# Attention B of three row blocks: head outputs kept turned, halves aligned by DMA, summed and scaled on GpSimd

## What is computed

```
score = sum_h w[t,h] * relu(q_idx[t,h] . k_idx[s])       # indexer
idx   = top_k(score, 256)                                # per row
logits[q,h,k] = q[h] . k[idx] / 8 + bias;  p = softmax(logits)
o_b   = p @ v                                            # 8 heads x 64
merged = sigmoid(gate_a) * (o_a @ w_branch_a) + sigmoid(gate_b) * (o_b @ w_branch_b)
x = x + merged @ w_out;  x = x + SwiGLU(rmsnorm(x));  out = rmsnorm(x)
```

## Time and profile before

| | before |
|---|---|
| median of 3 runs | 3301.77 us (3299.1 to 3305.61) |
| profiled execution | 3303.4 us, its span 3301.5 us |
| PE busy in the span | 3218.6 us, 97% |
| DVE, ACT, POOL busy | 59%, 44%, 55% |
| mean granted TensorE clock | 0.995 |

### The profile page before, as it was taken

One profiled execution on the slowest core, in us unless ns is written; L12 is line 12 of the kernel. 1 busy time (PEld: TensorE's weight loads), 2 busy tenths in 40 slices (PEclk: granted clock), 3 DMA queues, 4 the chain that ended last, 5 costly groups with the idle time before them and its releaser, 6 DMA issues.

```text
span 3301.5 us, 43302 instructions
## 1 busy us (share of the span) xinstructions
PE 3218.6 (97%) x15976; PEld 2698.9 (82%) x15976; DVE 1937.2 (59%) x3494; ACT 1441.6 (44%) x2610; POOL 1809.6 (55%) x1261
## 2 busy tenths in 40 slices
PE   8999999999999999999999999999999999999998
PEld 6888878878888888888888888888888789888887
DVE  3236747648565656567676766767868778621112
ACT  3324435435453544345454535736655367420001
POOL 5555554454455666645666664166666721566665
PEclk9999999999999999999999999999999999999999
DMA  5745454355524333323433332063333400433332
GB/s 160 204 138 173 115 165 138 105 152 154 190 79 147 108 112 97 118 90 120 162 103 107 96 119 93 1 233 100 101 96 116 157 18 1 137 118 96 96 102 96
DMA packets 446561, 388.98 MB, mean 118 GB/s; under 512 B 20976, under 2 KB 376560, under 8 KB 445712
## 3 DMA queue, kind: packets, MB, share of 16 engines
q1 hardware_dynamic: 424912, 341.99, 34.0%
q10 hardware_dynamic: 21440, 44.22, 3.6%
HBM read 323.37 MB, written 62.78 MB: 117 GB/s over the span
## 4 chain that ended last, share of the span: by engine, by line
PE 88%; DVE 4%; ACT 3%; POOL 2%; issue 2%; DMA 1%; ACTq 0%; SPq 0%; DVEq 0%; POOLq 0%
PE BANK L913 20%; PE BANK L914 20%; PE BANK L915 20%; PE LP L913 3%; PE LP L914 3%; PE LP L915 3%; PE BANK L1138 3%; PE LP L1122 2%; PE BANK L1153 2%; PE LP L1023 2%; PE LP L1022 2%; PE LP L1123 2%; PE BANK L1155 2%; POOL WLO L863 1%; PE BANK L1164 1%
## 5 line engine op out<-in xcount | busy, mean ns | idle before, releaser
L863 POOL TENSOR_TENSOR WLO<-WRAW,WHI 128x1024 fp32r<-128x1024 f32 x456 | 1107.1, 2428 | 38.0
L861 POOL TENSOR_SCALAR WHI<-WRAW 128x1024 fp32r<-128x1024 f32 x456 | 506.4, 1111 | 1036.7 <-PE BANK L915 846.0
L913 PE MATMUL BANK<-H2hi,WHI 128*128 128x512 f32 x1376 | 542.9, 395 | 6.8 <-ACT SL L1716 4.4
L914 PE MATMUL BANK<-H2lo,WHI 128*128 128x512 f32 x1376 | 538.4, 391 | 0.0
L915 PE MATMUL BANK<-H2hi,WLO 128*128 128x512 f32 x1376 | 537.7, 391 | 0.0
L913 PE MATMUL BANK<-HThi,WHI 128*128 128x512 f32 (+1 forms) x1024 | 404.5, 395 | 2.6 <-DVE QS L1782 2.6
L914 PE MATMUL BANK<-HTlo,WHI 128*128 128x512 f32 (+1 forms) x1024 | 400.0, 391 | 0.0
L915 PE MATMUL BANK<-HThi,WLO 128*128 128x512 f32 (+1 forms) x1024 | 400.0, 391 | 0.0
L1515 ACT ACTIVATE MASK<-SCD,THR 128x896 bf16<-128x896 f32 (+5 forms) x186 | 281.9, 1516 | 249.0 <-DVE THR L1842 221.4
L913 PEld LDWEIGHTS BANK<-H2hi,WHI 128*128 128x128 f32 x1376 | 259.9, 189 | 60.4 <-ACT SL L1716 4.8
L915 PEld LDWEIGHTS BANK<-H2hi,WLO 128*128 128x128 f32 x1376 | 259.6, 189 | 55.5
(11 more groups left out here) (294 smaller groups left out, 6666.8 us busy)
## 6 DMA issues: line engine op xcount, KB each, us to landing
WRAW<-in_w_in SPq DMA_DIRECT2D x124, 512.0 KB, 4.4
WRAW<-in_w_ffn_gate SPq DMA_DIRECT2D x88, 512.0 KB, 3.8
WRAW<-in_w_ffn_up SPq DMA_DIRECT2D x88, 512.0 KB, 3.8
WRAW<-in_w_ffn_down SPq DMA_DIRECT2D x88, 512.0 KB, 3.5
qsp<-QS SPq DMA_DIRECT2D x32, 512.0 KB, 5.7
gates<-GS ACTq DMA_DIRECT2D x64, 256.0 KB, 2.2
WRAW<-in_w_out SPq DMA_DIRECT2D x32, 512.0 KB, 4.2
GL<-gates ACTq DMA_DIRECT2D x48, 256.0 KB, 4.3
```

The lines of the kernel that those rows point to most:

```text
L861: nc.gpsimd.tensor_scalar(hi, raw, 1.0, 1.0, ALU.mult, ALU.mult).then_inc(w_hi, 1)
L863: nc.gpsimd.tensor_tensor(lo, raw, hi.bitcast(f32), ALU.subtract).then_inc(w_split, 1)
L913: nc.tensor.matmul(dst, whi, mhi, start=first, stop=False)
L914: nc.tensor.matmul(dst, whi, mlo, start=False, stop=False)
```

## The change

For blocks 1 to 3 the turn to [rows, d] and back falls away. XV stays in [d, rows]. Four SP DMAs for each quad (`shift_halves`) bring the half that lies in the wrong partitions to XZ and the half that is in place to OTB; POOL adds the two and multiplies by the inverted sums (`fold`). The sums lie in [rows, heads] and are needed along the free axis in all 64 partitions of a head: one DMA writes them to memory (`hand_sums`), two more read them back as a broadcast (`load_sums`). The last quad takes another way: ACT copies its upper half to the lower partitions, and DVE adds and scales it (`fold_last`). `sums_at` sets the slots of `whole_sums` and `invert` before the end of the quad. Block 0 stays as it was.

```diff
+        LASTQ = PAIRS // 2 - 1
+        def sums_at(b, kind, q):
+            if b == 0:
+                return quad_end(b, kind, q) + 2
+            count = len(groups(b, kind, 2 * q + 1))
+            return first_at(b, kind, 2 * q + 1) + (4 if count > 6 else 3 if count > 4 else 1)
...
+            def hand_sums(b, q):
+                j, g = q // 2, q % 2
+                sp.wait_ge(inverted, n(inverted, (b, "b", q)))
+                made(sum_out, (b, q), 16)
+                sp.dma_start(io["rsd"][b, j, 4 * g:4 * g + 4, :].rearrange("h r -> r h"), RS[:, j, 4 * g:4 * g + 4],
+                             allow_slow_non_contiguous=True).then_inc(sum_out, 16)
+            def load_sums(b, q):
+                j, g = q // 2, q % 2
+                sp.wait_ge(sum_out, n(sum_out, (b, q)))
+                if q >= 2:
+                    sp.wait_ge(o_scaled, n(o_scaled, (b, q - 2)))
+                made(sum_in[q % 2], (b, q), 32)
+                for s in range(2):
+                    sp.dma_start(RR[q % 2][s * HD:(s + 1) * HD, :, :],
+                                 io["rsd"][b, j, 4 * g:4 * g + 4, :].rearrange("(e s) r -> s e r", s=2)[s].partition_broadcast(HD)
+                                 ).then_inc(sum_in[q % 2], 16)
+            def shift_halves(b, q):
+                sp.wait_ge(x_copied, n(x_copied, (b, "b", q)))
+                if q >= 2:
+                    sp.wait_ge(o_scaled, n(o_scaled, (b, q - 2)))
...
+                for s in range(2):
...
+                    sp.dma_start(XZ[q % 2][r, :, :], other).then_inc(x_shifted[q % 2], 16)
+                    sp.dma_start(OTB[r, 2 * g:2 * g + 2, j * P:(j + 1) * P], own).then_inc(x_shifted[q % 2], 16)
...
                 if key == ("br", b, 1, 1):
+                    for q in range(LASTQ - 1) if b else ():
+                        hand_sums(b, q)
+                        load_sums(b, q)
+                        shift_halves(b, q)
                     last = units(b, "b")[-1]
                     sp.wait_ge(masked, n(masked, (last, chunks_of(last)[-1][0])))
...
+                    if b:
+                        hand_sums(b, LASTQ - 1)
+                        load_sums(b, LASTQ - 1)
+                        shift_halves(b, LASTQ - 1)
+                        hand_sums(b, LASTQ)
+                        load_sums(b, LASTQ)
...
+                def fold(q):
+                    j, g, s = q // 2, q % 2, q % 2
+                    pool.wait_ge(x_shifted[s], n(x_shifted[s], (b, q)))
+                    o = OTB[:, 2 * g:2 * g + 2, j * P:(j + 1) * P]
+                    nc.gpsimd.tensor_tensor(XZ[s][:, :, :], XZ[s][:, :, :], o, ALU.add).then_inc(o_added, made(o_added, (b, q)))
+                    pool.wait_ge(o_added, n(o_added, (b, q)))
+                    pool.wait_ge(sum_in[s], n(sum_in[s], (b, q)))
+                    nc.gpsimd.tensor_tensor(o, XZ[s][:, :, :], RR[s][:, :, :], ALU.mult).then_inc(o_scaled, made(o_scaled, (b, q)))
...
-                        if i == quad_end(b, kind, q):
+                        if i == (sums_at(b, kind, q) - 1 if b else quad_end(b, kind, q)):
                             whole_sums(kind, q)
...
+                    for q in range(LASTQ) if b else ():
+                        if i == quad_end(b, "b", q) + 5:
+                            fold(q)
...
-                branch(b, 0, 0, tail)
+                branch(b, 0, 0, None if b else tail)
...
+                    if b and q == LASTQ:
+                        nc.scalar.copy(XV[q % 2][0:HD, :, :], in_tiles(BANK[0])[HD:P, :, :]
+                                       ).then_inc(x_copied, made(x_copied, (b, kind, q)))
+                        return
...
+                def fold_last():
+                    s, rows = LASTQ % 2, slice((JT - 1) * P, JT * P)
+                    dve.wait_ge(x_copied, n(x_copied, (b, "b", LASTQ)))
...
+                    for i in range(2):
+                        last = nc.vector.tensor_tensor(OTB[i * HD:(i + 1) * HD, 2:4, rows], x[:, :, i, :], low[:, :, i, :], ALU.add)
+                    last.then_inc(o_folded, made(o_folded, b))
+                    dve.wait_ge(o_folded, n(o_folded, b))
+                    dve.wait_ge(sum_in[s], n(sum_in[s], (b, LASTQ)))
+                    nc.vector.tensor_tensor(OTB[:, 2:4, rows], OTB[:, 2:4, rows], RR[s][:, :, :], ALU.mult
+                                            ).then_inc(o_last, made(o_last, b))
...
-                        if i == quad_end(b, kind, q) + 2:
+                        if i == sums_at(b, kind, q):
                             invert(kind, q)
-                        if i == quad_end(b, kind, q) + 3:
+                        if b == 0 and i == quad_end(b, kind, q) + 3:
                             scale_heads(kind, q)
+                if b:
+                    fold_last()
                 for e in range(ET):
                     split_low(e)
```

More of the change, by code:

```diff
@@ L174, in trunk_program @@
         OTB = at("OTB", [P, ET, ROWS], f32, r3)
+        XZ = [at(f"XZ{i}", [P, 2, P], f32, r3 + 28672 + 1024 * i) for i in range(2)]
+        RR = [at(f"RR{i}", [P, 2, P], f32, r3 + 30720 + 1024 * i) for i in range(2)]
         SCD = at("SCD", [P, JT, SEQ], f32, rX)
@@ L238, in trunk_program @@
         o_step, o_ready, ot_ready = sem("o_step"), sem("o_ready"), sem("ot_ready")
+        sum_out, o_added, o_scaled, o_folded, o_last = (sem(s) for s in ("sum_out", "o_added", "o_scaled", "o_folded", "o_last"))
+        sum_in, x_shifted = [sem(f"sum_in{i}") for i in range(2)], [sem(f"x_shifted{i}") for i in range(2)]
         oh_ready, os_ready = sem("oh_ready"), [sem(f"os_ready{s}") for s in range(2)]
@@ L660, in load_tables @@
                 load_table(1, TABB, tabb_in, 0)
+            def hand_sums(b, q):
[18 more added lines that the diff above has]
+                    sp.wait_ge(o_scaled, n(o_scaled, (b, q - 2)))
+                made(x_shifted[q % 2], (b, q), 64)
+                j, g = q // 2, q % 2
+                for s in range(2):
+                    own, other = (XV[q % 2][i * HD:(i + 1) * HD, :, :].rearrange("d (e s) r -> d e s r", s=2)[:, :, s, :]
+                                  for i in (s, 1 - s))
+                    r = slice(s * HD, (s + 1) * HD)
+                    sp.dma_start(XZ[q % 2][r, :, :], other).then_inc(x_shifted[q % 2], 16)
+                    sp.dma_start(OTB[r, 2 * g:2 * g + 2, j * P:(j + 1) * P], own).then_inc(x_shifted[q % 2], 16)
             def first_attention(t):
@@ L1144, in values @@
                     if g == 0 and p % 2 == 0:
-                        values.bank = take("values", x_copied, (b, kind, p // 2), ("v", b, kind, p // 2))
+                        kept = (o_folded, b) if b and p // 2 == LASTQ else (x_copied, (b, kind, p // 2))
+                        values.bank = take("values", *kept, ("v", b, kind, p // 2))
                         if kind == "b" and p == 0:
@@ L1190, in attend @@
                         values(*seq[i])
-                    for kind, q in quads(b):
+                    for kind, q in quads(b) if b == 0 else ():
                         if i == quad_end(b, kind, q) + 1:
@@ L1421, in x_copy @@
                     act.wait_ge(values_done, n(values_done, last_group(b, kind, 2 * q + 1)))
-                    if quads(b).index((kind, q)) >= 2:
+                    if b and q >= 2:
+                        act.wait_ge(o_added, n(o_added, (b, q - 2)))
+                    elif b == 0 and quads(b).index((kind, q)) >= 2:
                         act.wait_ge(trans_full, n(trans_full, ("x", b) + quads(b)[quads(b).index((kind, q)) - 2]))
+                    if b and q == LASTQ:
+                        nc.scalar.copy(XV[q % 2][0:HD, :, :], in_tiles(BANK[0])[HD:P, :, :]
+                                       ).then_inc(x_copied, made(x_copied, (b, kind, q)))
+                        return
                     nc.scalar.copy(XV[q % 2][:, :, :].rearrange("p h q -> p (h q)"), BANK[0][:, :]
@@ L1445, in attend @@
                         nc.scalar.copy(PThi[r][:, 0:w, :], trans(key)[:, 0:w, :]).then_inc(pt_hi, made(pt_hi, key))
-                    for q in range(1, PAIRS // 2, 2):
+                    for q in range(1, PAIRS // 2, 2) if b == 0 else ():
                         for kind in kinds(b):
@@ L1638, in _ @@
                     pass
-                act.wait_ge(ot_ready, n(ot_ready, (b, "b", JT - 1)))
+                if b == 0:
+                    act.wait_ge(ot_ready, n(ot_ready, (b, "b", JT - 1)))
                 for e in range(ET):
+                    if b and e == 0:
+                        act.wait_ge(o_scaled, n(o_scaled, (b, LASTQ - 1)))
+                    if b and e == 2:
+                        act.wait_ge(o_last, n(o_last, b))
                     split_head(b, 1, e)
@@ L1950, in invert @@
                     nc.vector.reciprocal(RS[:, j, hs], RS[:, j, hs]).then_inc(inverted, made(inverted, (b, kind, q)))
+                def fold_last():
+                    s, rows = LASTQ % 2, slice((JT - 1) * P, JT * P)
```

(6 more changed lines are left out.)

## The result

The changed kernel took 3377.7 us (median of 4 runs, 3371.8 to 3382.9) against 3301.5 us for the kernel before, measured beside it: a ratio of 1.0226, 95% interval 1.0214 to 1.0238. The forecast was 3292 us, range 3279 to 3304. It was wrong in sign and in size: 76 us slower.

The account below looks back on a forecast made before the run. PE sets the pace in blocks 1 and 3, sharing it in block 2 with the DVE, POOL and ACT loop. -18.3 + 1.5 + 2.7 + 1.1 + 0.8 + 1.5 = -10.7 us, giving 3292 us, range 3279 to 3304.

Parts of the forecast that it names:

- The landing of `hand_sums`: Store of the sums on SP's queue: estimated to land in 2.7 us, between 2.2 and 3.5, like the other DMAs.
- Slower: Rival: shifts landing over 6.4 us make POOL's fold hold the negated maxima; 3346 us at 8.5 us landings; chance 0.11.
- The empty queue: Argument against the slower rival: SP's queue is empty when the shifts are issued, DMA share 0.03 to 0.04.
- A quad needs 0.44 + 2.7 + 0.9 + 1.8 us of SP: SP's queue for each quad: store issue, landing, reads and shifts fit into the shortest quad, 6 slots or 9 us.
- The removed matmuls: Blocks 1 to 3 away from the ends: turn-backs and transposes worth 21.5 us on PE, counted at 90, 75, 90%: -18.3 us.
- Folds: POOL away from the ends: folds of 1.35 us fit into its gaps; +1.5 us for those that hold a negation.
- The ends: Serial chain after each block's last negated maximum: +2.7 us in block 2, +1.1 in block 3, +0.8 in block 1.
- just in time: End of block 2: quad 7's sums out at 16.0, in at 19.0, first OTlo at 20.2 us, product starting at 20.65.
- 5.2 us for the first landing: Block ends, from the last negated maximum: `hand_sums(6)`, issued behind GL's 1.76 us, lands at about 5.2 us.
- The clock: Longer PE waits in blocks 2 and 3 may bring the 1.2 GHz level once more: +1.5 us, between 0 and 3.4.
- Full gain: Rival: no waits at the ends and all removed work counts, as DVE and ACT have room; 3277 to 3284 us; chance 0.18.

Follow-up runs that it names:

- runs of 16 bytes: The changed kernel with the store of the sums in 128 runs of 16 bytes instead of 512 single elements, reads unchanged: 3303.2 us, ratio 1.0004.
- the kernel without memory: The changed kernel without store and reads of the sums; fold and last scaling multiply the tile by itself: 3288.1 us, ratio 0.9958.
- late sums: The changed kernel without store and reads of the sums, and with sums completed and inverted at their places before the change: 3284.5 us, ratio 0.9945.

## Why the prediction was wrong

**The landing of `hand_sums`: the step that failed.** I took 2.7 us for each DMA alike, "my estimate between 2.2 us (256 KB to memory) and 3.5 (4 KB in runs of one element)". From its issue to the reads it measured 8.1 to 11.0 us over the 24 quads: 8.3 for the first, 10.1 behind the gates of block 2. Neither bounding row had the form of this store: one was 256 KB to memory, and G was a load. The 8.5 us of the other row of that load was the nearest number, and I gave it to the "Slower" rival at 0.11, with "nothing but that row" for it. The empty queue that I set against it (DMA share 0.03 to 0.04) was no argument: the share during the slow store is 0.03 too. Window of the first store after, same columns:

```profile
1452.40:1460.40 8.00, 7.37 (x52) 6.58 (x52) 6.08 (x19) 6.52 (x15) 3.62 (x8) 1.00 0.03 0
```

A store can take 8 us with nearly idle DMA engines. The Trainium skill's rule ("DMA: Bandwidth & Descriptors", "Rules for kernel authors") of one descriptor for each element pointed the right way, and the packets agree: 478241 after, 469025 with runs of 16 bytes, 24 x 384 fewer. The 2.0 us of fixed cost, which the prediction took from the same page, stand there in a section on DMAs that GpSimd issues; these are SP's, and rows of single numbers took 3.1 to 8.6 us at the median here. The number of packets alone does not set the time: 128 that lie apart land in 1.4 to 2.4 us away from the gates, 128 side by side take 7.2 at the median.

**What stands behind it.** "A quad needs 0.44 + 2.7 + 0.9 + 1.8 us of SP and the shortest takes 6 slots, 9 us" held with 2.7. With 0.4 + 8.3 + 1.3 + 2.6 it needs 12.6 us, more than any quad of block 1 lasted (8.5 to 12.3 from one copy of XV to the next), so the queue runs ever later there: up to the seventh copy of XV +20.4 us in block 1 and +6.7 in block 2, but -4.5 in block 3, where a quad lasts 20 us. The rival "Slower" had the last link of this (POOL's fold holds the negated maxima) and 3346 us, but from late landings of the shifts. The shifts landed in 2.5 us, near my 2.7; they were issued late, because they stood behind the store and the reads. It came to 3378 us.

**The removed matmuls, -18.3 us.** PE's busy time fell by 21.7 us in the kernel without memory (3218.6 to 3196.9), where I had 21.5. With the late sums the whole kernel is 17.7 us faster, with the cost of shifts and folds already in it. The size is about right, the division was not: in that kernel the middles gain 3.8, 4.3 and 6.5 us (I had 6.5, 5.4, 6.5), and the rest comes at the ends.

**Folds, +1.5 us.** An operation takes 0.73 us (I had 0.68), and without memory (late sums) the folds wait 4.9 us in 7 waits for the shift. Right in kind. The early sums, some 3.6 us if that difference holds, I had at nothing.

**The ends, +4.6 us.** Too small even for a good store. In the kernel with runs of 16 bytes, at the end of block 2, counted from the issue of GL (2144.10), the shift's last DMA was issued by 10.3 us where I had 7.9, and `fold(6)` began at 11.8. SP:

```profile
2144.10 1.75 SPq L769 DMA_DIRECT2D GL<-gates  x4
2145.89 0.43 SPq L680 DMA_DIRECT2D rsd<-RS  x1
2149.72 1.25 SPq L691 DMA_DIRECT2D RR<-rsd  x2
2151.07 0.61 SPq L706 DMA_DIRECT2D XZ<-XV  x1
...
2153.80 0.61 SPq L707 DMA_DIRECT2D OTB<-XV  x1
```

A shift DMA takes 0.61 us to issue, a read of the sums 0.63, where I had 0.44 from GL. The waits had the names that I gave (reciprocal for POOL, PE for PTlo in blocks 2 and 3, for OTlo in block 1), and with the true store they were 12.0, 10.1 and 16.4 us instead of about 4, 2.7 and 2.4. In blocks 2 and 3 PE then waited once more, 5.5 and 6.4 us for OTlo, where I had the sums of quad 7 "just in time": a second store in series. `fold(6)` waited 8.6, 10.0 and 9.1 us for its shift, where I had some 3. (My 5.2 us for the first landing is also 0.3 us more than 1.76 + 0.44 + 2.7.)

**The clock, +1.5 us.** The granted clock was 0.92, 0.95 and 0.97 over the three stretches where it had been 1.00, 0.99 and 0.99. Part of that fell on PE's waits and cost nothing; the rest shows in its busy time, 3208.0 us after and 3196.9 without memory for the same 15736 records: 11 us. It went with the waits: without memory and with late sums, where most of them are gone, it is 1.00 in all three. Mis-sized with them.

**A misreading.** DVE's share in the earlier trace rows is 81, 77 and 83%, not "68 to 83": 67.76 is its busy time in us in block 1. So DVE had a sixth to a quarter of each stretch free, less than the rival "Full gain" was given. No term of the sum rests on it.

## What to carry to other kernels

A small DMA must be priced by its form, not its bytes. If no row has the same direction, the same run on both sides and the same order over partitions, take the worst neighbour for the sum and not for the rival. Where one queue carries store, wait, read and an unrelated transfer in turn, the wait is paid by the unrelated one and by all that waits for it; put the waiting pair last. A detour through memory to get numbers across partitions is cheap in the middle of a loop and dear at its end, where it stands in series: keep the old way for the last items.

## What the runs showed of the hardware

- Small stores to memory with one piece from each partition, us from issue to landing at the median: 128 pieces of 16 bytes side by side 1.4; 128 of 8 bytes side by side 2.9; of single numbers side by side, one row of 32 3.1, four rows of 32 3.9, one row of 64 6.7, one row of 128 7.2, four rows of 128 8.6; 128 single numbers 16 bytes apart 1.8, 128 bytes apart 1.4. Why 64 cost nearly as much as 128, and why the distance in memory counts, stays open.
- A store of numbers side by side in flight delays what stands behind it on its queue, up to an issue of 3.28 us for a DMA that takes 0.61, though the DMA engines' share is 0.03.
- Half tiles of 64 KB between SBUF places landed in 2.0 us (2.5 with slow stores about), and took 0.61 us each to issue.
